# Values stage of a retrieval block: dense products for 192 of 256 tokens, gathered rows for the other 64

## The chip, the cores and the metric

The kernel runs on one core of one Trainium2 chip. The metric is the device time of one execution in microseconds (us). TensorE multiplies, ScalarE (ACT in the rows), VectorE (DVE) and GpSimd (POOL) compute and copy, and SyncE (SP) issues most transfers. In the rows PE is TensorE's matmul and PEld its weight load.

## The reference

One layer of a hybrid encoder on x of 256 tokens by 2048, all float32: token mixing (attention and retention heads), layer norm, retrieval of experts, layer norm. The change lies in the retrieval:

```
def peer_ffn(x, w_pq, sub_keys, expert_u, expert_v):
    ...
    best, pos = lax.top_k(cand, PEER_TOPK)                     # 16 experts for each of 8 heads
    expert_idx = jnp.take_along_axis(cand_idx, pos, axis=-1)   # of 16384 experts
    gate = jax.nn.softmax(best, axis=-1)
    ...
        u = jnp.take(expert_u, idx_b, axis=0)
        act = jax.nn.gelu(jnp.einsum('thkd,td->thk', u, xb), approximate=False)
        v = jnp.take(expert_v, idx_b, axis=0)
        return jnp.einsum('thk,thkd->td', g_b * act, v)
```

So each token takes 8 x 16 = 128 rows of `expert_v` (16384 rows of 2048), each with a weight gate x gelu(u . x). Then `layer_norm(ALPHA * x + ffn)`.

## The kernel before

The kernel doesn't gather. It works over all 16384 experts densely, in 128 tiles of 128 experts, for all 256 tokens. The gates are scattered into a table in DRAM that is zero elsewhere, and the weight of every expert for every token is gelu(score) x gate.

**Exact products from rounded operands.** TensorE is fed in the type fp32r. To keep float32's precision each operand is split: a high part (ScalarE's copy to fp32r) and a low part (the operand less its high part, by VectorE). A product is three matmuls, high x high, high x low and low x high, into one accumulator: the helper `three` (L443 to L445).

**Score stage** (to about 1274 us). For each tile, `expert_u` is loaded by SyncE, transposed by VectorE, split by ScalarE and VectorE, and multiplied with all tokens. ScalarE applies gelu and `wexp[:, tile, 0:256]` holds the result, experts on the partitions. Two tiles are a pair, 64 pairs in all. From pair 18 on GpSimd is free of splitting: it scatters the gates, 256 indirect transfers (`scatter`, L1818), each for 128 tokens of one block (b = 0 or 1) and one pick. Then it loads the gates of a pair (`load_gates`, L1834, two buffers) and multiplies them into `wexp` (`apply_gates`, L1842).

**Values stage** (from 1274 us). For each tile of 128 experts:
- SyncE loads the tile of `expert_v` in two halves of 1024 columns (`v_half`, L334, 512 KB each) into `raw`, four buffers. A buffer is reloaded when VectorE has split it.
- ScalarE copies the tile's weights (128 x 256) to `whalf_hi` (L1079) and each quarter (128 x 512) of the values to `split_hi` (L781), four slots. It waits until TensorE has used the slot.
- VectorE makes `whalf_lo` (L1635) and `split_lo` (L1134).
- TensorE (`value_tile`) takes each quarter for two blocks of 128 tokens, three matmuls each. Eight PSUM banks hold the sums of 2 blocks x 4 quarters over the whole stage.

Two tiles are a turn of each engine's loop. The last four tiles (`HELD`) are split into buffers of their own, so that block 0's products (`held_tile`) can all come before block 1's. **The end**: for each block VectorE adds ALPHA x residual to the sums (`summed`, L1669), takes statistics (L1672), GpSimd raises the variance to -0.5 (L1784), VectorE normalises (L1692, L1694), with some pieces by ScalarE (L1115) and GpSimd (L1776, L1777); SyncE stores eight pieces.

Each engine runs its own list in the order in which it is written, and the engines wait for each other through semaphores. An instruction that waits holds up all that stand behind it on its engine.

## Time and profile before

| | |
|---|---|
| device time, three runs | 1986.82, 1987.72, 1988.07 us, median 1987.72 |
| profiled execution | span 1986.6 us (the page states no other time of it) |
| TensorE | 99% of the span, 9838 matmuls |
| VectorE, ScalarE, GpSimd | 74%, 52%, 41% |
| DMA | 412 MB, 207 GB/s over the span |
| values, `expert_v` | 256 loads of 512 KB |
| gates | 64 loads of 256 KB |

The span runs from the first to the last instruction. The busy share of an engine is an average over stages; what bounds a stage is read from the waits in it. TensorE is the engine that waits for nobody over most of the span.

### The profile page before, as it was taken

The numbers are of one execution on the slowest core, as the hardware profiler recorded it, in microseconds if no ns is written. First come the engines' busy times: TensorE is split into PE (matmuls) and PEld (weight loads), VectorE is DVE, ScalarE is ACT, GpSimd is POOL, SyncE is SP. The second block draws the span as 40 slices with busy tenths as digits, with TensorE's granted clock in tenths as the row PEclk, the third lists the DMA queues.
The fourth block names the chain that finished last, engine by engine and source line by source line (L and its number), as shares of the span: only waits on it lengthen the run. The fifth ranks groups of instructions, "written<-read, shape, count | busy, mean of one in ns | idle before, by whom it ended". The sixth has DMA issues, their size and how long they took to land.

```text
span 1986.6 us, 37625 instructions
## 1 busy us (share of the span) xinstructions
PE 1965.2 (99%) x9838; PEld 1668.8 (84%) x9838; DVE 1478.3 (74%) x2406; ACT 1030.8 (52%) x1962; POOL 824.4 (41%) x614
## 2 busy tenths in 40 slices
PE   9999999999999999999999999999999999999996
PEld 8888888887888888888888888888888888888885
DVE  4555776766889889999999999877765555555556
ACT  4555555554655555444444444555555555555553
POOL 0000330201889998888888887456520000000001
PEclk9999999999999999999999999999999999999998
DMA  7787775676587767999999998878766555677563
GB/s 249 233 278 277 231 235 161 195 222 177 172 204 189 188 191 172 186 188 190 187 187 187 190 188 188 240 269 279 270 225 193 192 193 194 232 216 213 194 194 129
DMA packets 300843, 412.19 MB, mean 207 GB/s; under 512 B 80256, under 2 KB 211456, under 8 KB 300160
## 3 DMA queue, kind: packets, MB, share of 16 engines
q1 hardware_dynamic: 258816, 394.76, 66.4%
q0 software_dynamic: 41984, 16.93, 7.8%
q8 instruction: 18, 0.29, 0.1%
q14 instruction: 25, 0.20, 0.0%
HBM read 390.46 MB, written 21.10 MB: 207 GB/s over the span
## 4 chain that ended last, share of the span: by engine, by line
PE 96%; DVE 3%; DMA 1%; ACT 0%; POOL 0%; issue 0%; SPq 0%; DVEq 0%; ACTq 0%
PE ps L690 24%; PE ps L443 19%; PE ps L445 19%; PE ps L444 19%; PE ps L696 12%; DVE split_lo L1134 0%; PE ps L433 0%; PE ps L660 0%; DVE x_cols L1356 0%; DMA raw<-in_expert_v 0%; DVE end_lo L1662 0%; DVE act_both L1147 0%; DVE stats L1672 0%; DMA x_nat<-in_x 0%; DVE ps L1669 0%; PE ps L494 0%
## 5 line engine op out<-in xcount | busy, mean ns | idle before, releaser
L1134 DVE TENSOR_TENSOR split_lo<-raw,split_hi 128x512 fp32r<-128x512 f32 x800 | 608.3, 765 | 415.2 <-ACT split_hi L781 413.5
L781 ACT ACTIVATE split_hi<-raw 128x512 fp32r<-128x512 f32 x840 | 529.8, 632 | 545.7 <-PE ps L445 536.4
L690 PE MATMUL ps<-act_both,split_hi 128*128 128x512 f32 x2048 | 513.4, 393 | 0.0
L1818 POOL DMA_INDIRECT gate_dram<-pick_n,places x256 | 398.3, 1556 | 81.2 <-issue 81.2
L690 PEld LDWEIGHTS ps<-act_both,split_hi 128*128 128x128 f32 x2048 | 368.8, 189 | 65.4
L443 PE MATMUL ps<-split_hi,whalf_hi 128*128 128x512 f32 x992 | 386.3, 389 | 0.0
L444 PE MATMUL ps<-split_lo,whalf_hi 128*128 128x512 f32 x992 | 386.3, 389 | 0.0
L445 PE MATMUL ps<-split_hi,whalf_lo 128*128 128x512 f32 x992 | 386.3, 389 | 0.0
L992 ACT ACTIVATE split_hi<-ps 128x512 fp32r<-128x512 f32 x368 | 209.2, 595 | 260.8 <-PE ps L696 259.4
L696 PEld LDWEIGHTS ps<-act_both,split_lo 128*128 128x128 f32 x2048 | 279.5, 191 | 19.9
L696 PE MATMUL ps<-act_both,split_lo 128*128 128x256 f32 x2048 | 286.0, 283 | 0.0
L443 PE MATMUL ps<-split_hi,act_both 128*128 128x512 f32 x688 | 274.9, 400 | 1.9 <-DVE act_both L1147 1.4
L1784 POOL TENSOR_TENSOR stats<-stats 128x1 f32<-128x1 f32 (+1 forms) x6 | 9.7, 1614 | 633.2 <-DVE stats L1678 504.9
L445 PE MATMUL ps<-split_hi,act_both 128*128 128x512 f32 x688 | 268.9, 391 | 0.0
L444 PE MATMUL ps<-split_lo,act_both 128*128 128x512 f32 x688 | 268.2, 390 | 0.0
L1400 DVE TENSOR_TENSOR split_lo<-ps,split_hi 128x512 fp32r<-128x512 f32 x368 | 243.2, 680 | 16.4 <-ACT split_hi L992 11.5
L1414 DVE STREAM_TRANSPOSE ps<-raw 128x1024 f32<-128x1024 f32 x184 | 231.6, 1259 | 6.7
L444 PEld LDWEIGHTS ps<-split_lo,whalf_hi 128*128 128x128 f32 x992 | 186.2, 188 | 38.6
L445 PEld LDWEIGHTS ps<-split_hi,whalf_lo 128*128 128x128 f32 x992 | 186.2, 188 | 38.6
L443 PEld LDWEIGHTS ps<-split_hi,whalf_hi 128*128 128x128 f32 x992 | 186.2, 188 | 38.6
L1799 POOL TENSOR_TENSOR split_lo<-u_cols,split_hi 128x512 fp32r<-128x512 f32 x144 | 184.9, 1307 | 19.6 <-ACT split_hi L992 18.7
L443 PEld LDWEIGHTS ps<-split_hi,act_both 128*128 128x128 f32 x688 | 129.4, 188 | 28.0 <-DVE act_both L1147 2.1
(183 smaller groups left out, 1569.4 us busy)
## 6 DMA issues: line engine op xcount, KB each, us to landing
raw<-in_expert_u SPq DMA_DIRECT2D x1024, 128.0 KB
raw<-in_expert_v SPq DMA_DIRECT2D x256, 512.0 KB
raw<-in_w_in SPq DMA_DIRECT2D x112, 512.0 KB
gate_dram<-zeros SPq DMA_DIRECT2D x32, 512.0 KB, 5.9
raw<-in_w_out SPq DMA_DIRECT2D x32, 512.0 KB
raw<-in_w_pq SPq DMA_DIRECT2D x128, 128.0 KB
gates<-gate_dram POOLq DMA_DIRECT2D x64, 256.0 KB, 4.5
gate_dram<-pick_n,places POOLq DMA_INDIRECT x256
```

What stands on the lines that cost most here:

```text
L443: nc.tensor.matmul(acc, l_hi, r_hi, start=first, stop=False)
L444: nc.tensor.matmul(acc, l_hi, r_lo, start=False, stop=False)
L445: return nc.tensor.matmul(acc, l_lo, r_hi, start=False, stop=last)
L690: return nc.tensor.matmul(ps[:, bank, :], split_hi[:, q % SPLITS, i * P:(i + 1) * P], act_both[:, k, :, :].rearrange("p a t -> p (a t)"), ...
L696: return nc.tensor.matmul(ps[:, bank, 0:SEQ], split_lo[:, q % SPLITS, i * P:(i + 1) * P], act_hi[:, k, :], start=False, stop=False)
L781: nc.scalar.activation(split_hi[:, q % SPLITS, :], raw[:, q // 2, q % 2, :], ACT.Copy).then_inc(hi_ready, 1)
L992: nc.scalar.activation(split_hi[:, q % SPLITS, :], src, ACT.Copy).then_inc(hi_ready, 1)
L1134: vec.tensor_tensor(split_lo[:, q % SPLITS, :], raw[:, q // 2, q % 2, :], split_hi[:, q % SPLITS, :].bitcast(f32), ALU.subtract).then_inc( ...
L1400: vec.tensor_tensor(split_lo[:, q % SPLITS, :], ps[:, 4 + q % 4, :], split_hi[:, q % SPLITS, :].bitcast(f32), ALU.subtract).then_inc(lo_re ...
L1414: vec.transpose(dst.rearrange("p a (c g i) -> p g (a c) i", g=4, i=32), raw[:, k, :, :].rearrange("p a (b c q) -> p (a b) c q", b=2, c=8)) ...
L1799: eng.tensor_tensor(split_lo[:, q % SPLITS, :], u_cols[:, q // 2, q % 2, :], split_hi[:, q % SPLITS, :].bitcast(f32), ALU.subtract).then_i ...
L1818: eng.indirect_dma_start(gate_dram, bass.IndirectOffsetOnAxis(ap=places[:, b, k:k + 1], axis=0), pick_n[:, 2, b, k:k + 1], None, compute_o ...
```

## The change

The 256 tokens become a block FULL of 128 (tokens 0 to 127) and a block PART of 128, whose tokens are treated by halves.

- **Tokens 128 to 191, dense with two matmuls.** The weights of these 64 tokens stand in one operand of 128 columns, 64 low parts and 64 high parts (`wsplit`, columns LOD to LOD + 128). It is multiplied with the high and with the low values. The upper 64 rows of the bank then hold the high weights' sum, the lower 64 rows that of the low weights. (The product low x low comes with it.) At the end the lower rows are moved to the upper partitions and added.
- **Tokens 192 to 255, gathered.** Their 64 x 128 = 8192 picked rows of `expert_v` are gathered by 64 indirect transfers of 128 rows (1 MB each) into three buffers `rows`. Partitions 0 to 63 take the first 64 picks of the 64 tokens and partitions 64 to 127 the others. VectorE adds weight x row to `row_sum`, in two additions of 1024 columns for each transfer, 128 in all. The gates of these tokens aren't scattered. Their activations are stored to DRAM by SyncE during the score stage (`store_act`, four pairs behind) and picked from there by 64 small indirect transfers; GpSimd multiplies them with the gates in groups of four (`weigh`).
- Weights are applied and split for 192 columns in place of 256. ScalarE makes two copies a tile (64 and 192 columns). Gate buffers are three, and GpSimd has 16 pairs done before the first gather; from then on it weighs one pair per row.
- At the end both halves of PART are brought to their places before the sum with the residual: ScalarE copies, SyncE moves, GpSimd adds.

In the diff `store_act` is SyncE's, `add_row`, `more_rows`, the loop, `places_out` and `summed` are VectorE's, `load_row` and what follows it GpSimd's, and the last part is ScalarE's, behind its last splits.

```diff
-            def value_tile(n0, t, first, last_tile):
+            def value_product(w, q, r_hi, r_lo, b, first, last):
+                acc = ps[:, b * 4 + q, :]
+                if b == FULL:
+                    return three(acc, w[:, HI0:HI0 + P], w[:, LO0:LO0 + P], r_hi, r_lo, first, last)
+                both = w[:, LOD:LOD + P]
+                nc.tensor.matmul(acc, both, r_hi, start=first, stop=False)
+                return nc.tensor.matmul(acc, both, r_lo, start=False, stop=last)
...
+            def store_act(pair):
+                sp.wait_ge(gelu_done, pair * 2 + 2)
+                sp.dma_start(act_tiles[:, bass.ds(pair * 2, 2), :], wexp[:, bass.ds(pair * 2, 2), DENSE:SEQ]
+                             ).then_inc(act_out, 16)
...
+            def add_row(m):
+                j, cols = m // 2, slice(m % 2 * 1024, m % 2 * 1024 + 1024)
+                if m % 2 == 0:
+                    dve.wait_ge(row_in[j % ROW_SLOTS], 16 * (j // ROW_SLOTS + 1))
+                    dve.wait_ge(weight_ready, j // W_GROUP + 1)
...
+                vec.scalar_tensor_tensor(out=row_sum[:, cols], in0=rows[j % ROW_SLOTS][:, cols], scalar=picked_w[:, j:j + 1],
+                                         in1=row_sum[:, cols], op0=ALU.mult, op1=ALU.add).then_inc(row_used, 1)
+            def more_rows(i, at):
+                turn = i - FIRST_STEP
+                due = turn >= 0 and (at < 2 or turn % 5 == 4)
+                if due and done < 2 * STEPS:
+                    add_row(done)
+                    done += 1
...
+            for i in range(loops):
                 split_w(i * 8, 1)
                 for q in range(4, 8):
                     split(i * 8 + Q_V, q)
+                    if q == 5:
+                        more_rows(i, 0)
+                more_rows(i, 2)
                 split_w(i * 8, 2)
                 for q in range(4):
                     split(i * 8 + (Q_V + 8), q)
+                    if q == 1:
+                        more_rows(i, 1)
...
             def places_out():
+                chain.step(vec.scalar_tensor_tensor(out=places_f[HB:P, 0, :], in0=pick_n[HB:P, 0, PART, :], scalar=float(P),
+                                                    in1=pick_n[HB:P, 1, PART, :], op0=ALU.mult, op1=ALU.add))
...
+                vec.tensor_copy(places_u[HB:P, :, :], places_f[HB:P, :, :]).then_inc(places_ready, 1)
...
             dve.wait_ge(x1_out, 16)
+            dve.wait_ge(picked_in, 64)
...
+                    def load_row(j):
+                        if j >= ROW_SLOTS:
+                            pool.wait_ge(row_used, 2 * (j - ROW_SLOTS) + 2)
+                        eng.indirect_dma_start(rows[j % ROW_SLOTS][:, :], None, v_rows,
+                                               bass.IndirectOffsetOnAxis(ap=picked[:, 0, j:j + 1], axis=0)
+                                               ).then_inc(row_in[j % ROW_SLOTS], 16)
...
+                    for pair in range(APPLIED_AHEAD):
+                        apply_gates(pair)
+                    pool.wait_ge(split_free, Q_V + SPLITS)
+                    for j in range(ROW_SLOTS):
+                        load_row(j)
+                    eng.memset(row_sum[HB:P, :], 0.0).then_inc(own_ready, 1)
...
+                    eng.tensor_scalar(row_sum[0:HB, :], row_sum[0:HB, :], ALPHA, None, ALU.mult).then_inc(own_ready, 1)
+                    pool.wait_ge(act_out, 16 * PAIRS)
+                    load_acts(0)
+                    weigh(0)
+                    load_acts(1)
+                    pair = APPLIED_AHEAD
+                    for k in range(W_GROUPS):
+                        for j in range(k * W_GROUP + ROW_SLOTS, min((k + 1) * W_GROUP + ROW_SLOTS, STEPS)):
+                            load_row(j)
+                            if pair < PAIRS:
+                                apply_gates(pair)
+                                pair += 1
+                        if k + 1 < W_GROUPS:
+                            weigh(k + 1)
+                        if k + 2 < W_GROUPS:
+                            load_acts(k + 2)
...
             def summed(b, q):
-                dve.wait_ge(values_ready, 4 * b + q + 1)
+                if b == PART:
+                    dve.wait_ge(own_rows, q + 1)
+                    dve.wait_ge(low_added, q + 1)
...
+            act.wait_ge(row_used, 2 * STEPS)
+            for q in range(2):
+                low_to_sbuf(q)
+            act.wait_ge(own_summed, 1)
+            for q in range(2):
+                own_to_psum(q)
+            for q in range(2, 4):
+                low_to_sbuf(q)
+            for q in range(2, 4):
+                own_to_psum(q)
```

Other places in words. In the last four tiles the weights are in `wend`, and PART's products come before FULL's. SyncE loads the residual of tokens 192 to 255 into `row_sum` at the start of the values stage, moves `row_sum`'s upper half down (`half_moved`) after the last value load, and moves the four pieces of low sums. `DENSE` is 192, `HB` 64, `STEPS` 64, `ROW_SLOTS` 3, `W_GROUP` 4, `FIRST_STEP` 2. VectorE's and GpSimd's loops of the values stage are written out.

TensorE in the values loop, the matmuls of one quarter. Before, `whalf_hi` and `whalf_lo` are the weights:

```order
L443 MATMUL ps<-split_hi,whalf_hi 128x512
L444 MATMUL ps<-split_lo,whalf_hi 128x512
L445 MATMUL ps<-split_hi,whalf_lo 128x512
L443 MATMUL ps<-split_hi,whalf_hi 128x512
L444 MATMUL ps<-split_lo,whalf_hi 128x512
L445 MATMUL ps<-split_hi,whalf_lo 128x512
```

After, L507 to L509 are `three` and L794, L795 the two with the mixed operand. One matmul of six is gone:

```order
L507 MATMUL ps<-split_hi,wsplit 128x512
L508 MATMUL ps<-split_lo,wsplit 128x512
L509 MATMUL ps<-split_hi,wsplit 128x512
L794 MATMUL ps<-split_hi,wsplit 128x512
L795 MATMUL ps<-split_lo,wsplit 128x512
```

VectorE in the values loop, one tile and the start of the next, before:

```order
L1635 TENSOR_TENSOR whalf_lo<-wexp,whalf_hi 128x256
L1133 REGISTER_ALU
L1134 TENSOR_TENSOR split_lo<-raw,split_hi 128x512
L1133 REGISTER_ALU
L1134 TENSOR_TENSOR split_lo<-raw,split_hi 128x512
L1133 REGISTER_ALU
L1134 TENSOR_TENSOR split_lo<-raw,split_hi 128x512
```

After, a turn with a third addition (L1751 is the addition, L1227 the split of the values, L1738 that of the weights; the number behind `rows` names the buffer):

```order
L1738 TENSOR_TENSOR wsplit<-wexp,wsplit 128x192
L1227 TENSOR_TENSOR split_lo<-raw,split_hi 128x512 x2
L1751 SCALAR_TENSOR_TENSOR row_sum<-rows_108,picked_w,row_sum 128x1024
L1227 TENSOR_TENSOR split_lo<-raw,split_hi 128x512 x2
L1751 SCALAR_TENSOR_TENSOR row_sum<-rows_108,picked_w,row_sum 128x1024
L1738 TENSOR_TENSOR wsplit<-wexp,wsplit 128x192
L1227 TENSOR_TENSOR split_lo<-raw,split_hi 128x512 x2
L1751 SCALAR_TENSOR_TENSOR row_sum<-rows_109,picked_w,row_sum 128x1024
```

An addition of 1024 columns now stands in the middle of each tile's four splits, and every fifth turn has one between the tiles.

GpSimd in the values stage, before:

```order
L1842 TENSOR_TENSOR wexp<-wexp,gates_59 128x512
L1843 REGISTER_ALU
L1834 ISA
L1834 DMA gates_59<-gate_dram 128x512
L1840 ISA
L1842 ISA
L1842 TENSOR_TENSOR wexp<-wexp,gates_60 128x512
L1834 ISA
L1834 DMA gates_60<-gate_dram 128x512
```

After, the border between two groups of four rows (L1999 gathers a row for each partition, L1990 and L1982 weigh a pair and load the gates of a later one, L2014 makes four weights of the next group, L2006 picks activations):

```order
L1999 DMA rows_107<-in_expert_v,picked 128x2048
L1990 TENSOR_TENSOR wexp<-wexp,gates_60 128x2x192
L1982 DMA gates_60<-gate_dram 128x2x192
L2014 TENSOR_TENSOR picked_w<-picked_act,picked_gate 128x4
L2006 DMA picked_act<-act_dram,picked 128x1 x4
L1999 DMA rows_108<-in_expert_v,picked 128x2048
```

The weights of a group now stand behind a gather and a gate multiply, and that gather waits until VectorE has used the row three before.

## Rows read from the trace of the kernel before

**Rows 1.** The page: span, TensorE's busy time, and the chain's shares by engine

```profile
span 1986.6 us, 37625 instructions
PE 1965.2 (99%) x9838; PEld 1668.8 (84%) x9838; DVE 1478.3 (74%) x2406; ACT 1030.8 (52%) x1962; POOL 824.4 (41%) x614
PE 96%; DVE 3%; DMA 1%; ACT 0%; POOL 0%; issue 0%; SPq 0%; DVEq 0%; ACTq 0%
```

**Rows 2.** Timeline, TensorE, first matmuls of the values stage and of its last tiles

```profile
1274.24 0.40 PE L443 MATMUL ps<-split_hi,whalf_hi 128*128 128x512 f32 x1
...
1948.82 0.40 PE L443 MATMUL ps<-end_hi,wend_hi 128*128 128x512 f32 x1
```

**Rows 3.** Busy time by stretch: score stage, values stage thrice; last PEclk, DMA share, GB/s

```profile
840.00:1240.00 400.00, 400.00 (x2294) 352.26 (x2293) 382.83 (x503) 196.39 (x428) 329.61 (x212) 1.00 0.93 188
1310.00:1400.00 90.00, 90.00 (x399) 74.53 (x398) 67.61 (x82) 47.35 (x83) 52.64 (x55) 1.00 0.82 274
1500.00:1600.00 100.00, 100.00 (x443) 82.81 (x442) 56.87 (x92) 52.64 (x92) 0.00 (x0) 1.00 0.59 193
1824.00:1828.00 4.00, 4.00 (x19) 3.31 (x18) 1.64 (x4) 2.01 (x5) 0.00 (x0) 1.00 0.95 357
```

**Rows 4.** Waits 1274 to 1948 us: who for whom, us in total, times, longest

```profile
ACT split_hi L781 <- PE ps L445: 313.4, 487, 0.8
DVE split_lo L1134 <- ACT split_hi L781: 252.3, 440, 1.8
```

**Rows 5.** Groups by line, VectorE's splits, 1274 to 1461 and 1461 to 1600 us

```profile
L1134 DVE TENSOR_TENSOR split_lo<-raw,split_hi 128x512 fp32r<-128x512 f32 x139 | 128.6, 934 | 47.0 <-ACT split_hi L781 46.4
...
L1134 DVE TENSOR_TENSOR split_lo<-raw,split_hi 128x512 fp32r<-128x512 f32 x103 | 72.0, 700 | 58.4 <-ACT split_hi L781 58.3
```

**Rows 6.** VectorE back to back (timeline), and L1346 by its line (ns min/median/max)

```profile
1944.85 1.43 DVE L1656 TENSOR_TENSOR wend_lo<-wexp,wend_hi 128x256 fp32r<-128x256 f32 x4
1946.19 4.90 DVE L1662 TENSOR_TENSOR end_lo<-raw,end_hi 128x512 fp32r<-128x512 f32 x8
...
L1346 DVE SCALAR_TENSOR_TENSOR x_nat<-x_nat,stats,ln_w x5: 744/1274/1282, 445.8 to 462.9; 128x1024 f32<-128x1024 f32 x3, 128x512 f32<-128x512 f32 x2
```

**Rows 7.** Timeline, GpSimd: the last of 256 indirect issues

```profile
1235.65 1.55 POOL L1818 DMA_INDIRECT gate_dram<-pick_n,places  x1 [0.30 <-issue]
```

**Rows 8.** Timeline of the same time: VectorE, then GpSimd

```profile
1339.05 2.17 DVE L1134 TENSOR_TENSOR split_lo<-raw,split_hi 128x512 fp32r<-128x512 f32 x2 [0.67 <-ACT split_hi L781]
...
1344.49 0.69 DVE L1134 TENSOR_TENSOR split_lo<-raw,split_hi 128x512 fp32r<-128x512 f32 x1 [0.33 <-ACT split_hi L781]
...
1338.78 1.28 POOL L1842 TENSOR_TENSOR wexp<-wexp,gates 128x512 f32 x1 [0.41 <-DMA gates<-gate_dram]
...
1344.28 0.55 POOL L1834 DMA_DIRECT2D gates<-gate_dram  x1 [0.67 <-DMA gates<-gate_dram]
```

**Rows 9.** DMA: GB/s in 1-us slices of 1790:1830; q0 in 840:1240; issues to landing

```profile
GB/s 115 225 258 94 238 228 203 76 54 202 221 246 373 385 360 283 221 127 303 123 209 246 111 250 188 98 279 227 156 61 58 190 165 176 336 393 397 303 295 90
...
q0 software_dynamic: 30768, 0.12, 20.7%
...
x_back<-x_dram SPq DMA_DIRECT2D x16, 128.0 KB, 4.2
...
ln2b<-in_ln_b SPq DMA_DIRECT2D x1, 1024.0 KB, 8.7
```

**Rows 10.** The tail: timeline of ScalarE and VectorE; GpSimd's groups by line

```profile
1956.95 2.42 ACT L1111 ACTIVATE end_hi<-raw 128x512 fp32r<-128x512 f32 x4 [2.49 <-DMA raw<-in_expert_v]
...
1960.09 0.69 DVE L1669 SCALAR_TENSOR_TENSOR ps<-x_back,ps 128x512 f32<-128x512 f32 x1
...
1965.54 0.26 DVE L1677 BATCH_NORM_AGGREGATE stats<-stats 128x2 f32<-128x24 f32 x1
...
L1776 POOL TENSOR_TENSOR y_out<-y_out,ln2w 128x512 f32<-128x512 f32 x3 | 3.8, 1281 | 2.7 <-ACT y_out L1115 2.7
...
L1784 POOL TENSOR_TENSOR stats<-stats 128x1 f32<-128x1 f32 x2 | 1.1, 558 | 504.9 <-DVE stats L1678 504.9
```

257 lines of the change are left out of this document (181 added, 76 removed).

## The prediction

> **What bounds the kernel now.** I read the head of the page first, then the chain that ended last, then the engines by stretch, then the waits. [rows 1]: TensorE is busy 99% of the span and is 96% of the chain, so in every long stage it sets the time. [rows 2]: the values stage begins at 1274.24 and its last tiles at 1948.82 us. In between stand 62 turns of two tiles, 48 matmuls each, 2976 in all, so one costs 674.58 / 2976 = 0.2267 us and a turn 10.88 us. [rows 3]: no stretch of it leaves TensorE idle and the granted clock is 1.00, the 2.4 GHz level, so nothing is to be had from the clock. VectorE is at 57% when GpSimd rests and 75% when GpSimd weighs gates; DMA is at 0.59 and 0.82 of its time. [rows 4]: the waits are the feeders' own: ScalarE waits 313.4 us for TensorE to free a slot, VectorE 252.3 us for ScalarE. TensorE waits for nobody. Fewer matmuls therefore mean a shorter stage, until one of the feeders is full.
>
> **What is removed.** Five matmuls per quarter in place of six: three for the 128 tokens, two for the 64. In the turns that is 62 x 8 = 496 fewer: 496 x 0.2267 = **-112.4 us**, a turn then takes 9.07 us. I assume that a matmul with the mixed weights costs what the others do, since its shape is the same. The last four tiles also lose 16 matmuls (3.6 us), but the first block's products there wait for the last operands: the last of VectorE's splits ends at 1960.1 [rows 10] and the second block's 48 products come after it either way. I count 0 and keep -3.6 as a bound.
>
> **What VectorE gets.** Work in a turn of 9.07 us: eight splits of 128x512. Back to back they take 4.90 / 8 = 0.61 us, alone 0.69 [rows 6, 5]. Two weight splits, 192 columns now; four of 256 take 1.43 us, 0.36 each, and by the columns 0.29. And 2.2 additions of 128x1024. The nearest row is the same operation and shape with its operands in SBUF, 1274 ns median [rows 6]; back to back less the same 0.08, so 1.20. Sum 8 x 0.61 + 2 x 0.29 + 2.2 x 1.20 = **8.1 us**; with every duration taken alone 8 x 0.69 + 2 x 0.35 + 2.2 x 1.27 = 9.0.
>
> On top comes GpSimd. [rows 5]: the same split takes 934 ns while gates are weighed and 700 after. [rows 8] show why: two splits that overlap a GpSimd multiply take 2.17 us, one that overlaps GpSimd's issue of a transfer takes 0.69, as always. So the multiply costs a busy VectorE some 0.7 us, the issue nothing. The multiply shrinks from 512 to 384 columns, 0.5 us of delay, 1.1 of them a turn: +0.55 us, in the 44 turns in which the 48 remaining pairs are weighed.
>
> A wait is added too. The weights of a group of four rows are multiplied by GpSimd only after it has waited for the last row of the group before to be used. Behind that stand a gather (1.55 + 0.30 us, the pace of indirect issues in [rows 7]), a gate multiply (1.28 for 512 columns [rows 8], about 1.0 for 384), the wait and the issue of a gate load (0.67 + 0.55 [rows 8]) and the weights' own multiply (0.56, a tiny one on GpSimd [rows 10]): 4.6 us. The next addition is due about 4.5 - 1.2 = 3.3 us after the last ended. VectorE, with the splits queued behind the addition, waits 1.3 us every 3.6 turns: +0.4 a turn. Together 8.1 + 0.55 + 0.4 = 9.07 us, all of the turn. VectorE is full, just.
>
> The Trainium skill has a rule against this edit: the page Vector Engine (DVE) Microarchitecture Reference, "Points that are easy to get wrong", says that this operation with two sources in SBUF that aren't bf16 runs at half throughput. By it an addition would cost 1.07 us more. The row of this kernel with two such sources disagrees: 1274 ns for 1024 columns is one column per 1.04 ns plus a start.
>
> **What the queues get.** A turn loads four blocks of 512 KB, 1.1 gathers of 1 MB and 1.1 gate loads of 192 KB: 2.10 + 1.15 + 0.22 = 3.47 MB, 382 GB/s at 9.07 us. Before, 274 GB/s is the most that any long stretch moves, at a share of 0.82; 357 GB/s stand in one of 4 us at 0.95 [rows 3]; slices of 1 us reach 385 and 397 [rows 9]. So DMA is nearly full too. At 375 GB/s, between the last two, a turn is 9.25 us. By the long stretch alone, 274 / 0.82 = 334 GB/s, it is 10.4; at 397 it costs nothing.
>
> Three resources at 97 to 100% don't mesh without loss, since a slot of four gives a split less than 2 us of slack (4 x 1.13, less 1.13 and the 1.4 of both splits). I take 9.4 us for the 44 turns with gates and 9.07 for the rest: 44 x 0.33 = **+14 us** (0 to +38 here; more is a rival).
>
> **Start of the additions: +3 us (0 to 7).** GpSimd issues its last scatter at 1235.65 [rows 7] and, two landings of some 4 us [rows 9] later, weighs 16 pairs at 2.2 us or more (1.0 + 0.67 + 0.55). It then issues three gathers, clears and scales the sum (2048 columns; at most 5.1 us for the scaling by the 1.28 of 512), issues four small gathers and waits for them: about 1304. VectorE comes to the first addition about 1295, with up to 2 us of slack. The scatters of the second block have half the rows; if that makes them shorter, the stall is gone.
>
> **Score stage: +1.5 us (0 to 6).** Three more small VectorE instructions and a wait for four copies. The stores of 64 tokens' activations (64 x 256 short packets) come into a stretch where DMA is at 0.93 and TensorE still has no gap [rows 3]; the scatters there, 20.7% of the 16 engines' time [rows 9], shrink by a quarter and make room.
>
> **Tail: +5 us (2 to 9).** Today VectorE begins the end of the first block at 1960.1 and is through at 1965.5 [rows 10]; from there it works without a gap. Now ScalarE copies the low half out, but only after its last splits (1956.95 + 2.42 [rows 10]), a transfer moves it across partitions (4.2 us, like the residual's [rows 9]), GpSimd adds it (1.3 a piece [rows 10]), four times. First sum about 1965, last 1970.7: 5 us late, and the second block stands behind it on VectorE.
>
> **Sum.** On the profiled span: 1986.6 - 112.4 + 14 + 3 + 1.5 + 5 = 1897.7; the median shown is 1.1 above that span, so **1899 us**.
>
> **Rivals.**
> - *TensorE stays the bound, the feeders keep up.* For it: with VectorE at 96% of the stretch 840 to 1240, TensorE has no gap there [rows 3]. 1987.7 - 112.4 + 5 = 1880, 1877 with the saving in the last tiles.
> - *The queues are the bound.* At 357 GB/s a turn is 9.72: 58 turns x 0.65 = 38 us in place of 14, 1923; at 334 GB/s 58 x 1.33 = 77, 1962. For it: no stretch longer than 4 us has shown more. Against: share and rate don't rise together, 1 us slices reach 397. The skill's HBM Reference ("Specifications (TRN2)") gives a core 358 GB/s as its share and about 425 when it streams alone. The one would be this rival at 1923, the other would leave DMA out of the matter; only one core runs here, and the 397 is above the share.
> - *Slower: the gathers' issue holds VectorE up.* No row shows VectorE reading two SBUF tensors beside an indirect issue of 1.55 us; the direct issue of 0.55 beside it costs nothing [rows 8]. There are 2.2 indirect issues a turn (a gather and an activation's per row). If each blocked VectorE in full, a turn were 9.07 + 3.4 = 12.5: 58 x 3.4 = 200 us, 2085 and slower. It turns into a loss from about 10.9 us a turn, 0.8 us per issue.
> - *The rows come too late.* Three slots of 8 KB give a gather two rows' time, 16.5 us; a load of 1 MB landed in 8.7 [rows 9]. Beyond some 18 us VectorE waits at each row; beyond 23 the gain is gone.
> - *The addition at half rate,* as the page has it: 128 x 1.07 = 137 us more on a full VectorE, 2035.
>
> **How the numbers follow.** Forecast 52%, TensorE bound 15%, queues 18%, issue 10%, late rows 4%, half rate 1%. The range is 1877 to 1962 us: both bounds of the DMA rate and the free case; it leaves the last three out. 0.2% (4 us) is about what a measurement can tell from no change. Faster 0.87, same 0.02, slower 0.11.
>
> **What would show it.** Matmuls of the stage still 0.227 us apart where they run, with 5 per quarter. TensorE with idle time released by VectorE's split, some 15 us in all, nearly all of it while gates are weighed. VectorE above 95% until then; its addition at 1.27 us. DMA share above 0.9. If ScalarE waits for the values' load instead, it is the queues; if splits take over 1 us after the last gate, it is the issue; if the addition waits for the row, the gather is late. A tail that is not longer, or a stall of tens of us at the first addition, would make terms wrong, not the sign.

## The result, and the profile after

The changed kernel takes 1973.0 us in the median of 4 runs (1968.5 to 1977.5), the kernel before 1987.9 (1986.8 to 1989.8). The ratio is 0.9926, 95% interval 0.9914 to 0.9937. So it is 15 us faster, where 89 were forecast, and outside the range of 1877 to 1962. The profiled execution is the slowest of the four, 1977.5 us with a span of 1975.7. I compare it with the span of 1986.6 before, so the rows account for 11 us of the 15 and show some 4 us more loss than the median has.

The head of the page and the chain's shares, which answer [rows 1]:

```profile
span 1975.7 us, 36205 instructions
PE 1887.2 (96%) x9326; PEld 1574.4 (80%) x9326; DVE 1600.8 (81%) x2538; ACT 1031.9 (52%) x2098; POOL 1002.3 (51%) x770
PE 66%; issue 12%; POOL 11%; DMA 4%; DVE 4%; SPq 2%; ACT 1%; POOLq 0%; ACTq 0%; DVEq 0%
```

TensorE has 512 matmuls less (9838 to 9326), 496 of them in the turns, as counted. But it is 66% of the chain and no longer 96%. The busy time by stretch, which answers [rows 3] (busy us and count of PE, PEld, DVE, ACT, POOL; then granted clock, DMA share, GB/s):

```profile
840.00:1240.00 400.00, 400.00 (x2295) 352.25 (x2294) 382.93 (x502) 196.83 (x429) 325.63 (x226) 1.00 0.92 195
1274.00:1300.00 26.00, 13.51 (x51) 10.65 (x50) 8.73 (x15) 7.71 (x19) 13.26 (x8) 0.74 0.82 263
1300.00:1740.00 440.00, 408.88 (x1717) 317.49 (x1716) 386.04 (x519) 243.31 (x516) 221.76 (x198) 1.00 0.93 333
1740.00:1860.00 120.00, 102.39 (x403) 80.02 (x402) 86.65 (x124) 56.70 (x121) 33.71 (x30) 0.91 0.90 292
1860.00:1930.00 70.00, 69.16 (x304) 56.56 (x303) 59.97 (x93) 43.64 (x97) 8.57 (x7) 1.00 0.86 308
```

The score stage is as it was. In the values stage TensorE is starved in three places: at the start (half idle, and the granted clock falls to 0.74), all through 1300 to 1740, and from 1740 to 1860, where the clock falls too. Only from 1860 on does it run nearly without a gap. The waits from 1310 to 1740 (who for whom: us in total, times, longest), which answer [rows 4]:

```profile
POOL rows L1999 <- DVE row_sum L1751: 181.5, 37, 9.6
ACT split_hi L851 <- PE ps L795: 98.3, 152, 5.3
ACT split_hi L851 <- DMA raw<-in_expert_v: 92.4, 54, 4.0
PEld ps L507 <- DVE split_lo L1227: 58.7, 74, 3.9
DVE split_lo L1227 <- ACT split_hi L851: 42.6, 45, 2.7
DVE row_sum L1751 <- issue: 7.6, 5, 3.5
```

ScalarE waits 92 us for the values' loads, and TensorE for VectorE. So no single engine is the bound. GpSimd and "issue" (time for which the profile names no releaser) together are 23% of the chain, but GpSimd isn't full either: of the 430 us it waits 181.5 for VectorE to use a row. A count makes the loss plain. VectorE splits every value once, 496 splits in the loop, eight to a turn, and at TensorE's pace of 9.07 us a turn a split stands for 1.134 us. The groups by line, 1310 to 1740 us and 1740 to 1860 us, which answer [rows 5]:

```profile
L1227 DVE TENSOR_TENSOR split_lo<-raw,split_hi 128x512 fp32r<-128x512 f32 x334 | 242.5, 762 | 42.8 <-ACT split_hi L851 42.6
L1751 DVE SCALAR_TENSOR_TENSOR row_sum<-rows,picked_w,row_sum 128x1024 f32<-128x1024 f32 x92 | 120.2, 1307 | 8.0 <-issue 7.6
...
L1227 DVE TENSOR_TENSOR split_lo<-raw,split_hi 128x512 fp32r<-128x512 f32 x82 | 56.3, 719 | 33.3 <-ACT split_hi L851 33.2
```

334 splits in 430 us are a turn of 10.30 us, and 430 - 334 x 1.134 = 51 us are lost. 82 splits in 120 us lose 27. From 1270 to 1310 there are 22 in 40 us, 15 lost, and some 3 are left for the time after 1860 and the borders between the stretches. With 5 us in the tail: 1986.6 - 112.4 + 15 + 51 + 27 + 3 + 5 = 1975. The forecast had +14 for meshing, +3, +1.5 and +5 in their place.

**The start.** SyncE's queue and, last, VectorE's first split after the gap:

```profile
1263.56 2.86 SPq L366 DMA_DIRECT2D raw<-in_expert_v  x2
1266.47 9.21 SPq L421 DMA_DIRECT2D act_dram<-wexp  x4
1275.78 13.26 SPq L441 DMA_DIRECT2D row_sum<-x_dram  x8
1289.41 2.17 SPq L366 DMA_DIRECT2D raw<-in_expert_v  x4
...
1294.05 3.02 DVE L1227 TENSOR_TENSOR split_lo<-raw,split_hi 128x512 fp32r<-128x512 f32 x4 [14.09 <-ACT split_hi L851]
```

The last four stores of activations and the eight loads of the residual are new on SyncE and stand ahead of the values' next loads. Together they hold its queue for 22.5 us, and VectorE idles for 14.1. Not all of it is issue: for 7.5 of the 9.2 us of the stores SyncE waits until ScalarE has made the last activations. VectorE has split the first slot's values at 1273, so what holds back its reload until 1289.4 is above all the residual's eight loads, 13.3 us; one of them alone takes 6.05.

**A group's weights.** VectorE, then GpSimd at the same time:

```profile
1458.50 1.32 DVE L1751 SCALAR_TENSOR_TENSOR row_sum<-rows,picked_w,row_sum 128x1024 f32<-128x1024 f32 x1 [3.55 <-issue]
...
1453.75 2.07 POOL L1999 DMA_INDIRECT rows<-in_expert_v,picked  x1 [3.94 <-DVE row_sum L1751]
...
1458.19 0.21 POOL L2014 TENSOR_TENSOR picked_w<-picked_act,picked_gate 128x4 f32<-128x4 f32 x1
```

The gather, the gate's multiply and the gate's load stand before the weights' multiply, 4.4 us, and the addition starts 0.1 us after it. This is the wait that the forecast took from the order of the code.

**The residual for the end.** The chain from 1737.5 us (start, us, what):

```profile
1737.52 0.38 SPq L463
...
1737.95 2.44 SPq L463
...
1740.43 3.67 SPq L463
...
1744.14 0.58 SPq L463
...
1745.08 3.21 SPq L366
...
1748.54 7.32 DMA raw<-in_expert_v
...
1755.96 0.64 ACT split_hi L851
```

Four loads of 128 KB, in pieces of 128 bytes, hold SyncE's queue for 7.2 us. The issue of the values' load behind them, 0.33 us otherwise, takes 3.21, and the transfer 7.32. ScalarE had waited for it.

**The tail.** SyncE, GpSimd, and VectorE's first sum, which answer [rows 10]:

```profile
1929.23 6.79 SPq L366 DMA_DIRECT2D raw<-in_expert_v  x5
1936.07 0.52 SPq L470 DMA_DIRECT2D row_half<-row_sum  x1
...
1945.91 4.58 POOL L2047 TENSOR_TENSOR row_sum<-row_sum,row_half 64x2048 f32<-64x2048 f32 x1 [49.60 <-DMA row_half<-row_sum]
...
1952.00 0.69 DVE L1807 SCALAR_TENSOR_TENSOR ps<-x_back,ps 128x512 f32<-128x512 f32 x1 [5.94 <-POOL x_back L2052]
```

From the end of the loop's splits (1929.2) to the end of the span are 46.5 us, before 41.7 (1944.9 to 1986.6): 4.8 more. VectorE idles 5.9 us before the first sum. GpSimd is late because the transfer of the sum's upper half was issued behind five of the values' loads and took 9.8 us.

### The profile page after: what moved, and what is told of

It is laid out like the page before. It is cut to its first block, busy times and chain, and to the rows that moved or that the text cites. A ratio compares the mean times of both kernels' runs of the same rounds, so it can differ in the third digit from the quotient of the medians.

```text
span 1975.7 us, 36205 instructions
## 1 busy us (share of the span) xinstructions
PE 1887.2 (96%) x9326; PEld 1574.4 (80%) x9326; DVE 1600.8 (81%) x2538; ACT 1031.9 (52%) x2098; POOL 1002.3 (51%) x770
## 4 chain that ended last, share of the span: by engine, by line
PE 66%; issue 12%; POOL 11%; DMA 4%; DVE 4%; SPq 2%; ACT 1%; POOLq 0%; ACTq 0%; DVEq 0%
PE ps L754 24%; PE ps L760 12%; PE ps L507 9%; PE ps L509 9%; PE ps L508 9%; POOL rows L1999 3%; DMA raw<-in_expert_v 3%; POOL wexp L1990 3%; POOL picked_act L2006 3%; POOL gates L1982 2%; DVE split_lo L1227 1%; SPq L463 1%; PE ps L795 1%; PE ps L794 1%; SPq L441 1%
## 5 line engine op out<-in xcount | busy, mean ns | idle before, releaser
L1227 DVE TENSOR_TENSOR split_lo<-raw,split_hi 128x512 fp32r<-128x512 f32 x800 | 585.0, 755 | 269.0 <-ACT split_hi L851 267.3
L851 ACT ACTIVATE split_hi<-raw 128x512 fp32r<-128x512 f32 x840 | 518.3, 629 | 533.7 <-PE ps L509 218.9
L1958 POOL DMA_INDIRECT gate_dram<-pick_n,places x256 | 380.4, 1486 | 78.1 <-issue 77.8
L760 PEld LDWEIGHTS ps<-act_both,split_lo 128*128 128x128 f32 x2048 | 279.5, 190 | 19.9
L507 PE MATMUL ps<-split_hi,act_both 128*128 128x512 f32 x688 | 274.7, 399 | 2.0 <-DVE act_both L1240 1.5
L509 PE MATMUL ps<-split_hi,act_both 128*128 128x512 f32 x688 | 268.7, 391 | 0.0
L507 PE MATMUL ps<-split_hi,wsplit 128*128 128x512 f32 x496 | 206.2, 416 | 62.1 <-DVE split_lo L1227 60.4
L1999 POOL DMA_INDIRECT rows<-in_expert_v,picked x64 | 92.2, 1441 | 296.7 <-DVE row_sum L1751 291.5
L508 PE MATMUL ps<-split_lo,wsplit 128*128 128x512 f32 x496 | 196.8, 397 | 0.0
L509 PE MATMUL ps<-split_hi,wsplit 128*128 128x512 f32 x496 | 196.4, 396 | 0.0
L794 PE MATMUL ps<-split_hi,wsplit 128*128 128x512 f32 x496 | 196.0, 395 | 0.0
L795 PE MATMUL ps<-split_lo,wsplit 128*128 128x512 f32 x496 | 195.5, 394 | 0.0
L1938 POOL TENSOR_TENSOR split_lo<-u_cols,split_hi 128x512 fp32r<-128x512 f32 x144 | 184.8, 1310 | 19.6 <-ACT split_hi L1062 18.9
L507 PEld LDWEIGHTS ps<-split_hi,wsplit 128*128 128x128 f32 x496 | 94.6, 191 | 113.0 <-DVE split_lo L1227 95.9
L1751 DVE SCALAR_TENSOR_TENSOR row_sum<-rows,picked_w,row_sum 128x1024 f32<-128x1024 f32 x128 | 166.2, 1298 | 9.2 <-issue 8.7
```

Source lines behind the costliest of these rows:

```text
L507: nc.tensor.matmul(acc, l_hi, r_hi, start=first, stop=False)
L508: nc.tensor.matmul(acc, l_hi, r_lo, start=False, stop=False)
L509: return nc.tensor.matmul(acc, l_lo, r_hi, start=False, stop=last)
L760: return nc.tensor.matmul(ps[:, bank, 0:SEQ], split_lo[:, q % SPLITS, i * P:(i + 1) * P], act_hi[:, k, :], start=False, stop=False)
L794: nc.tensor.matmul(acc, both, r_hi, start=first, stop=False)
L795: return nc.tensor.matmul(acc, both, r_lo, start=False, stop=last)
```

## The experiments

In the table are the splits of VectorE in three stretches of each profile, read like the rows above. In brackets stands what the stretch lost against 1.134 us a split. In e4, e9, e10 and e13 TensorE has less to do, so a loss there can be below 0. Those four, e1 and e2 ran once, e5, e6 and e7 twice, the others four times. The four runs of a kernel lie 4 to 12 us apart, and each kernel has one profile: the changed kernel, e5, e6 and e7 of their slowest run, e8 of its fastest. A difference of a few us, or of 3 or 4 splits, therefore proves nothing by itself.

| kernel | time, us | 1270 to 1310 | 1310 to 1740 | 1740 to 1860 |
|---|---|---|---|---|
| after | 1973.0 | 22 (15) | 334 (51) | 82 (27) |
| e1 thin additions | 1937.6 | 22 (15) | 355 (27) | 94 (13) |
| e2 quarter rows | 1935.9 | 20 (17) | 352 (31) | 102 (4) |
| e5 both | 1912.6 | 21 (16) | 366 (15) | 106 (0) |
| e4 two products of five out | 1962.4 | 25 (12) | 331 (55) | 93 (15) |
| e9 e1 and e4 | 1934.0 | 24 (13) | 352 (31) | 92 (16) |
| e10 e2 and e4 | 1927.7 | 23 (14) | 349 (34) | 106 (0) |
| e13 e10, quarter loads | 1911.7 | 25 (12) | 358 (24) | 113 (-8) |
| e6 whole pieces | 1964.8 | 21 (16) | 334 (51) | 90 (18) |
| e7 no gates' multiply | 1965.0 | 19 (18) | 341 (43) | 84 (25) |
| e3 start order | 1968.6 | 26 (11) | 332 (54) | 92 (16) |
| e8 merged | 1954.4 | 29 (7) | 336 (49) | 96 (11) |
| e11 merged, quarter loads | 1936.4 | 27 (9) | 341 (43) | 102 (4) |
| e12 quarter loads alone | 1964.5 | 21 (16) | 340 (44) | 85 (24) |

### e1 and e2: VectorE or the queues

e1, the additions over 8 columns:

```
-                j, cols = m // 2, slice(m % 2 * 1024, m % 2 * 1024 + 1024)
+                j, cols = m // 2, slice(m % 2 * 1024, m % 2 * 1024 + 8)
```

> The changed kernel, with each of VectorE's 128 additions over 8 columns in place of 1024 (so the sum of the gathered rows is left out for the other columns); all gathers and waits as they are. It takes some 150 us of work off VectorE and no byte off DMA. Theory A (the queues bound the stage, at about 340 GB/s): no more than 15 us faster than the changed kernel's 1973 us, ScalarE still waits over 120 us for the values' load. Theory B (VectorE is full): 1890 to 1910 us, and the waits for the load go to nearly nothing.

e2, only every fourth row gathered:

```
+                        if j >= ROW_SLOTS and j % 4:
+                            eng.dma_start(rows[j % ROW_SLOTS][:, 0:8], v_rows[0:P, 0:8]).then_inc(row_in[j % ROW_SLOTS], 16)
+                            return
                         eng.indirect_dma_start(rows[j % ROW_SLOTS][:, :], None, v_rows,
```

> The changed kernel, with only every fourth gather carried out; in place of the others GpSimd issues a load of 32 bytes per partition into the same buffer, so those rows' sums are left out. VectorE's additions keep their full size. It takes some 46 of 67 MB off DMA. Theory A (queues): 1905 to 1925 us, that is, all but the stall at the start of the stage and the tail comes back, and ScalarE waits less than 40 us for the values' load. Theory B (VectorE is full): within 15 us of 1973.

Measured: 1937.6 and 1935.9 us, 35 and 37 less than 1973. Both expectations of both runs missed. Neither VectorE nor the queues is the bound alone. The two profiles in the stretch 1300 to 1740, e1 then e2:

```profile
1300.00:1740.00 440.00, 425.82 (x1818) 340.48 (x1818) 312.81 (x552) 255.72 (x545) 194.72 (x207) 0.99 0.96 354
```

```profile
1300.00:1740.00 440.00, 422.20 (x1803) 333.70 (x1802) 410.03 (x545) 262.28 (x541) 211.60 (x203) 1.00 0.80 269
```

With thin additions the queues go to a share of 0.96. With fewer rows VectorE goes to 410 of 440 us. Each takes up what the other gave.

### e5: both reliefs

Both edits together.

> Both reliefs at once: the additions cover 8 columns in place of 1024, and after the first three only every fourth row is gathered (the rest are 32-byte loads), so the result lacks most of the picked rows' sum. Each alone gave about 36 us (1937.6 and 1935.9). Theory: VectorE and the DMA queues are both near full and each keeps the other from making good a delay, so together they give back nearly all of what the forecast missed: a turn of 9.1 to 9.3 us, TensorE bound, 1893 to 1908 us with the late start and the slow stretch from 1740 to 1860 left in. Rival: something that neither relieves (GpSimd's multiply on the gates, the order on SyncE, the 128-byte pieces) holds the turn at 9.4 to 9.7 us: 1920 to 1935.

Measured: 1912.6 us (1910.8 and 1914.5), between the two ranges, nearer to the theory's. The stretches 1300 to 1740 and 1740 to 1860:

```profile
1300.00:1740.00 440.00, 431.16 (x1868) 351.26 (x1868) 320.32 (x567) 270.28 (x559) 181.98 (x211) 0.99 0.83 278
1740.00:1860.00 120.00, 119.64 (x528) 98.68 (x528) 83.00 (x160) 76.63 (x158) 18.15 (x23) 1.00 0.79 262
```

From 1740 on there are 106 splits in 120 us, a turn of 9.06 us: TensorE's own pace, as the forecast had it. So the saving of 112.4 us is real. SyncE's short pieces are still there, and cost nothing when VectorE and the queues have room. The table says which of the two matters more here: with fewer rows alone (e2) the stretch loses 4 us, with thin additions alone (e1) 13. What is left is the start (16 us), 15 us from 1310 to 1740, and the tail.

### e4: TensorE relieved

```
-                    for b in range(TB):
+                    for b in ([FULL, PART] if first else [FULL]):
```

> The changed kernel without the two matmuls for the 64 mixed tokens in the loop after its first tile, so their sums are left out: three matmuls per quarter, 24 x 0.227 = 5.4 us a turn in place of 9.07. All loads, splits and additions stay. Theory A (queues at 340 GB/s, 3.47 MB a turn): a turn can't get below some 9.7 to 10 us, the time stays within 30 us of 1973. Theory B (VectorE, 8.1 us of work a turn and more with GpSimd beside it): 40 to 90 us faster. If the queues lose only by their meshing with TensorE's pace, also faster, with a rate of over 370 GB/s over the stage.

Measured: 1962.4 us, 11 less, in one run. From 1310 to 1740 there are 331 splits, no more than in the changed kernel (334). The 11 us lie within the 30 that the theory of the queues allowed, and outside the 40 to 90 of the other. TensorE's 9.07 us don't hold that stretch at all.

### e9 and e10: each of the two by itself

e9 is e1 and e4 together: only the queues are left near a limit. e10 is e2 and e4 together: only VectorE.

> The queues measured by themselves: additions over 8 columns, and the two products of the low and high weights left out in the loop, so that VectorE has some 6.5 us and TensorE 5.4 us of work in a turn while all loads and gathers stay (the result lacks both parts). Theory (the queues carry 355 to 365 GB/s at most when both kinds of load are always waiting): 3.47 MB take 9.5 to 9.8 us, 350 to 362 splits from 1310 to 1740 us, as with thin additions alone (355), 1925 to 1938 us. Rival (the forecast's 375 GB/s or more was there and the other engines kept the queues from it): 372 splits or more, below 1915.

> VectorE measured by itself: every fourth row gathered after the first three (other rows: 32-byte loads), and the two products of the low and high weights left out in the loop; the additions are whole (the result lacks both parts). DMA has 2.6 MB a turn and TensorE 5.4 us of work. Theory (the forecast's sum for VectorE, 9.07 us a turn with GpSimd's multiply and the wait for a group's weights, is about right, and quarter rows alone were slower because three engines near their limits disturb one another): 362 to 379 splits from 1310 to 1740 us, 1900 to 1920 us. Rival (VectorE's own work is longer than summed, 9.7 us a turn): 350 to 356 splits, as with quarter rows alone (352), 1928 to 1938.

Measured: 1934.0 and 1927.7 us. e9, the DMA view from 1310 to 1740, and from the waits of the same stretch ScalarE's for loads:

```profile
DMA packets 45196, 154.00 MB, mean 358 GB/s; under 512 B 14272, under 2 KB 14272, under 8 KB 38790
```

```profile
ACT split_hi L851 <- DMA raw<-in_expert_v: 142.1, 77, 5.8
```

e9's theory held. With nothing else to wait for, the queues carry 358 GB/s, 352 splits, a turn of 9.77 us. e1 has 355 splits, so thin additions alone had already brought the kernel to the queues' limit. In e10 neither held, but the rival missed by very little (349 splits against 350 to 356, 1927.7 us against 1928 to 1938, a turn of 9.86 us). But its rows don't say that VectorE's work is that long (stretch, then wait):

```profile
1300.00:1740.00 440.00, 315.31 (x1079) 210.28 (x1078) 399.52 (x544) 247.76 (x540) 238.13 (x202) 0.92 0.79 268
```

```profile
ACT split_hi L851 <- DMA raw<-in_expert_v: 108.8, 69, 5.9
```

VectorE is busy 399.5 of 440 us, and ScalarE waits 109 us for loads although the queues are at 0.79. That left open what holds a turn when both have room.

### e11, e12, e13: when a load is released

A values' load of 512 KB fills one of four slots, and is issued when both splits of the slot's last content are done. The edit loads quarters of 256 KB, each as soon as its own split is done, with a second set of semaphores for the odd quarters:

```
-                sp.dma_start(raw[:, slot, :, :].rearrange("p a b -> p (a b)"),
-                             v_v[bass.ds(j * P, P), hf * 1024:hf * 1024 + 1024]).then_inc(raw_ready[slot], 16)
+                for a in range(2):
+                    if free is not None:
+                        sp.wait_ge(lo_ready, free + a)
+                    sp.dma_start(raw[:, slot, a, :], v_v[bass.ds(j * P, P), hf * 1024 + a * COLS:hf * 1024 + a * COLS + COLS]
+                                 ).then_inc((raw_ready, raw_odd)[a][slot], 16)
```

e11 has it on the merged kernel (e8, below), e12 on the changed kernel, e13 on e10.

> Complete kernel, on top of the merged one (1954.4 median): the values' loads come as 256 KB (512 columns, 2 KB pieces) in place of 512 KB, each issued as soon as its own quarter is split instead of when both are. Theory (the loss from 1310 to 1740 is a lack of slack: a load has 6 us between its slot's release and its use, and lands in 5 to 6 us while a gather runs): a load gets a split's time more, 1.1 us, 345 to 355 splits there in place of 336, 1937 to 1948 us. Rival (queues near their ceiling and shorter pieces cost them more than slack gives): at most 338 splits, 1953 us or more.

> Complete kernel: the changed kernel with the values' loads in quarters of 256 KB (2 KB pieces) as its only edit. On the merged kernel the same edit took 18 us (1954.4 to 1936.4). Theory (a good part of what the change fails to bring is lost because a values' load is released too late, in every stretch of the stage): 12 to 22 us less than 1973, 1951 to 1961. Rival (in the merged kernel the quarters helped because the start, the residual's loads and the weights were already out of the way): 1966 or more.

> VectorE alone, as in the tenth run (a quarter of the rows gathered, two products of five left out, whole additions: 349 splits from 1310 to 1740 us, 1927.7 us), with the values' loads in quarters of 256 KB. There VectorE was busy 399.5 of 440 us although the queues were at 0.79 and TensorE had little to do. Theory (VectorE's own work fits in 9.1 to 9.3 us a turn, the rest of the 9.86 is loads released late): 365 splits or more, VectorE busy over 415 of 440 us, 1900 to 1912 us. Rival (VectorE's instructions and waits themselves take the 9.86 us): at most 355 splits, 1920 us or more.

Measured: e11 1936.4 us (1936.1 to 1946.9), 18 less than e8, better than its theory's range in time and short of it in splits (341). e12 1964.5 (1962.5 to 1966.1), 8.5 less than the changed kernel: a clear gain, since its slowest run is faster than the changed kernel's fastest, but between the theory's 12 to 22 and the rival's bound of 7. e13 1911.7, 16 less than e10, in one run, in the theory's range (1900 to 1912) by a hair; its 358 splits lie between the two, and VectorE's 413.9 us just under the 415. e13, the stretch and the waits:

```profile
1300.00:1740.00 440.00, 318.71 (x1107) 208.87 (x1105) 413.91 (x561) 260.63 (x553) 248.72 (x209) 0.94 0.86 275
```

```profile
ACT split_hi L855 <- DMA raw<-in_expert_v: 66.1, 49, 5.5
DVE row_sum L1757 <- issue: 14.4, 8, 2.3
```

The same work takes 9.61 us a turn in place of 9.86, and ScalarE's wait falls from 109 to 66 us. Why it matters is seen best in the chain of the merged kernel from 1740 us:

```profile
1740.17 8.19 DMA raw<-in_expert_v
...
1748.47 0.64 ACT split_hi L864
...
1749.13 1.31 DVE split_lo L1240 x2
...
1750.45 9.16 DMA raw<-in_expert_v
```

VectorE's splits release a slot, the load takes 8.19 us to land, two splits follow, and the slot is released again, 10.28 us after the first time. No engine works without a break in that loop. The four slots are used once a turn, so a turn can't be shorter than one slot's round. At 9.07 us the round leaves 7.1 us for issue and landing. The loads in the chain take 7.3 to 9.4 us in the changed kernel (six of them from 1748 to 1868 us), 6.1 to 13.0 in the merged one (from 1328 us on). From 1300 to 1740 us the merged kernel's chain is 31% such loads and 23% splits. The chain picks out the slow loads, and the profile gives no landing time for all of the 512 KB loads, so what share of the rounds is too long stays open. The quarters of e11 land in 6.4 us (median of all) and start a split earlier. The edit changes two things at once, the time of the release and the size of a load, and no run has one without the other; nor did any run have a fifth slot.

### e3, e8: a mended start, and the merged kernel

e3 puts the values' loads ahead of the stores and the residual's pieces on SyncE, one of each in turn, weights the first group before the sum is scaled, and lets the additions begin in turn 4:

```
-            for pair in range(PAIRS - STORE_LAG, PAIRS):
-                store_act(pair)
...
+                v_half(i * 2 + n // 2, n % 2, n)
+                if i == 1:
+                    store_act(PAIRS - STORE_LAG + n)
...
+                own_piece(RAWS * (i - 1) + n)
```

> The changed kernel with another order at the start of the values stage: SyncE issues each load of values of the first two turns ahead of one of the last activation stores and one piece of the residual, GpSimd picks and multiplies the first weights before it scales the sum, and the additions start two turns later (a third one in every fourth turn). Theory: the 14 us in which ScalarE waits for the first reload of the values after 1280 us, behind 13 us of residual pieces on SyncE, go; 1957 to 1963 us if nothing takes its place. Rival (the stage is bound by DMA bytes alone, so the loads only come later): 1968 to 1978, no change.

Measured: 1968.6 us in the median, but 1962.7 to 1974.9, so 4.4 less than the changed kernel, which the spread of both doesn't tell from nothing; two runs of four came near the expected 1957 to 1963, two did not. In its profile the start loses 11 us in place of 15: the loads are ahead now, but each residual piece still holds SyncE between two of them.

e8 adds three things: the weights one row into the group before, the residual's 16 loads one by one between the values' loads, and the sum's upper half ahead of the last four loads:

```
-                        if k + 1 < W_GROUPS:
-                            weigh(k + 1)
+                            if j == k * W_GROUP + ROW_SLOTS and k + 1 < W_GROUPS:
+                                weigh(k + 1)
...
+                v_half(i * 2 + k // 2, k % 2, k)
+                if n % 2:
+                    back_piece(n // 2)
...
+                if n == 4:
+                    sp.wait_ge(row_used, 2 * STEPS)
+                    sp.dma_start(row_half[0:HB, :], row_sum[HB:P, :]).then_inc(half_moved, 16)
```

> Complete kernel. On top of the start order of the third experiment (1968.6 median, 1961.9 span of the profile): a group's weights are multiplied one row into the group before instead of at its end; the residual's 16 loads are issued one by one between the values' loads instead of four in a row; the row that carries the upper half of the sum is issued before the last four values' loads. Theory: the wait for a group's weights goes (about 9 us of VectorE's idle time, half of which shows), the stretch 1740 to 1860 gains 5 to 8 us, the tail 3 to 5: 1950 to 1957. Rival: queues and VectorE stay full, only the tail gains: 1962 to 1967.

Measured: 1954.4 us (1949.0 to 1960.4), ratio to the kernel before 0.9837 (0.9810 to 0.9865). The time is in the theory's range, but not all of its parts came. The tail gained 0.5 us and not 3 to 5: from the end of the loop's splits to the end of the span are 45.9 us (1901.3 to 1947.2), against 46.4 in e3. The sum's upper half comes sooner, but it is put ahead of the last four values' loads, and VectorE's last split ends 19.9 us after the loop's, 3 us later than in e3. From 1310 to 1740 us VectorE has no wait for a group's weights left. Yet the stretch has 336 splits, hardly more than 334. The wait had been 7.6 us, but the loads are as late as before (ScalarE waits 86.0 us for them, against 92.4), and 6.0 us of idle time before splits, for which the profile names no releaser, are new. The start loses 7 us and the stretch from 1740 on 11.

e11, on top of it, has the ratio 0.9758 (0.9729 to 0.9786): 51 us faster than the kernel before and 37 faster than the changed one. Its stretches:

```profile
1300.00:1740.00 440.00, 417.76 (x1754) 323.63 (x1752) 407.95 (x530) 253.78 (x526) 232.95 (x201) 1.00 0.97 342
1740.00:1860.00 120.00, 117.30 (x505) 93.58 (x505) 106.27 (x156) 73.72 (x152) 35.92 (x31) 1.00 1.02 357
```

### e6 and e7: two smaller causes

e6, the residual's loads in long pieces:

```
-                        sp.dma_start(natural[:, r, :, :], strided(x1_dram[of_rows, b, cols])[:, r, :, :]
+                        sp.dma_start(x1_back[to_rows.start + r * n:to_rows.start + r * n + n, b, cols], v_v[r * n:r * n + n, cols]
```

> The residual's 16 loads for the end, which come in pieces of 128 bytes, are replaced by 16 loads of the same size in pieces of 4 KB from the values' first rows (wrong content, same bytes). In the changed kernel the stretch 1740 to 1860 us has 82 splits of VectorE, against 93 at the pace of the stretch before it. Theory (the short pieces occupy the queues, and SyncE's 1.3 to 1.8 us an issue hold back the values' loads behind them): 91 to 95 splits there and 10 to 15 us less, 1958 to 1963. Rival (it is their bytes, or the two tables of 1 MB before them): at most 85 splits there and within 4 us of 1973.

e7, the gates' multiply in 4 columns:

```
-                        part = wexp[:, 2 * pair:2 * pair + 2, 0:DENSE]
+                        part = wexp[:, 2 * pair:2 * pair + 2, 0:DENSE if pair < APPLIED_AHEAD else 4]
...
```

> GpSimd's multiply on the gates covers 4 of 192 columns in the 48 pairs of the values stage; the gates' loads stay, the result lacks those gates. With the multiply VectorE's splits take 762 ns on average from 1310 to 1740, without it about 690. Theory (the multiply's hold on VectorE is a part of the loss): 334 x 0.07 = 23 us less work for VectorE and, since the queues hold the other part, 8 to 20 us faster: 1953 to 1965. Rival (the queues set the pace there): within 5 us of 1973.

Measured: e6 1964.8 us (1959.9 and 1969.7), 90 splits from 1740 to 1860. That is inconclusive: e3 and e4, with their short pieces in place, have 92 and 93 there, and e7 and e12 84 and 85. So kernels whose edits lie elsewhere differ here by 10 splits, 11 us. That may be scatter from run to run and most of the spread between a kernel's runs; no kernel was profiled twice, so it isn't shown. What e6 does show is the issue. SyncE's instruction in the changed kernel and in e6 (ns min/median/max):

```profile
L463 SPq DMA_DIRECT2D x_back<-x_dram x16: 382/754/3666, 1737.5 to 1816.4; - x16
```

```profile
L463 SPq DMA_DIRECT2D x_back<-in_expert_v x16: 337/431/1530, 1739.5 to 1809.7; - x16
```

e7 gave 1965.0 us (1960.6 and 1969.4), 8 less, at the edge of the theory's range; its slower run lies among the changed kernel's. The splits take 686 ns in place of 762 from 1310 to 1740, 341 of them. GpSimd's multiply does slow VectorE, but is at most a small part of the loss. The splits and the stretch:

```profile
L1227 DVE TENSOR_TENSOR split_lo<-raw,split_hi 128x512 fp32r<-128x512 f32 x341 | 222.3, 686 | 74.3 <-ACT split_hi L851 64.9 <-issue 8.5
```

```profile
1310.00:1740.00 430.00, 404.70 (x1718) 320.41 (x1717) 348.97 (x520) 239.28 (x513) 179.03 (x195) 0.99 0.95 345
```

## Why the prediction was wrong, point by point

- **TensorE's saving, -112.4 us: right.** 496 matmuls fewer, and e5 has the turn of 9.06 us in its last stretch. TensorE is simply no longer what sets the pace.
- **VectorE's work in a turn: 3% short.** Forecast 8.65 us busy and 0.4 of waiting for weights, 9.05 (the forecast writes 9.07). In the changed kernel it is 386.0 / 440 x 10.30 = 9.04 busy and 7.6 us / 41.75 turns = 0.18 waiting, and with the most room (e13) 9.04 and 0.32. So a turn takes up to 9.36 us for VectorE, not 9.07. That is 13 us over 44 turns. The term that was too small is GpSimd's multiply. In e7, nearly without it, VectorE is busy 349.0 of 430 us, 8.19 us a turn of 10.09: the 8.1 for its own work held, and the multiply costs some 0.9 us where 0.55 was put.
- **The addition at half rate: didn't happen.** The 92 additions from 1310 to 1740 us take 1307 ns on average. By the rule of the Trainium skill it would have been 1.07 us more (Vector Engine (DVE) Microarchitecture Reference, "Points that are easy to get wrong"); these rows don't bear it out.
- **The issue of gathers holding up VectorE, and rows too late: didn't happen.** In e7, nearly without the multiply, the splits are at 686 ns beside all those issues, and in the changed kernel they are at 687 from 1770 on, after the last gate's multiply. All six waits before an addition end 0.1 us after the weights' multiply, and no row shows an addition waiting for its row.
- **The queues' rate: the step that failed by its number.** "At 375 GB/s, between the last two" took the rate from slices of 1 us. Held for 430 us with both kinds of load always waiting, it was 358 (e9), a turn of 9.77 us in place of 9.25. The bytes were right: 144.8 MB in 41.75 turns are 3.47 MB each. Over the 44 turns that load gates the half microsecond is 23 us. The rival at 357 GB/s, 1923 us with a chance of 18%, had the rate right. Its 38 us counted gate loads in all 58 turns; without them a turn has 3.25 MB, 9.1 us at that rate, so the rate alone costs 44 x 0.70 = 31 us, the loss that e9 shows. The Trainium skill's HBM Reference ("Specifications (TRN2)"), which gives a core a share of 358 GB/s, has the same figure; I had set it against a slice of 397. That section of the Trainium skill also gives about 425 for a core that streams alone; here it wasn't reached, though the queues' share in e9 was 0.97. That one core alone stops there for that reason isn't shown by any run.
- **The +14 us for the turns with gates (0 to 38): the term that failed most, by the rate and by meshing.** From 1310 to 1740 the loss is 51 us. The 14 were 44 x 0.33, of which 0.18 a turn, 8 us, stood for the queues' rate and 6 for meshing. If the queues' 31 are taken off the 51, some 20 are left for meshing: so 23 of the 37 us of error are the rate's and 14 meshing's. That division is an estimate. With TensorE relieved, the queues alone lose 31 there (e9), VectorE alone 34 (e10), and the two together 55 (e4). I read it so: a delay by one isn't made good while the other is near its limit. The forecast had seen that "a slot of four gives a split less than 2 us of slack" and priced it as small. It had not written down the round of a slot: release, issue, landing, two splits. It knew no landing time of a values' load, and took none. e11, e12 and e13 show that smaller loads, released earlier, gain 18, 8.5 and 16 us with the same work, and that even so 24 to 44 of the us up to 1740 stay lost.
- **The start, +3 us: wrong by 12, and the step missing.** I followed GpSimd's queue and not SyncE's. The diff puts 12 transfers ahead of the values' loads there. They hold its queue for 22.5 us, 13.3 of them with the residual's pieces. The +3 had been for the first addition, before which VectorE shows no idle time.
- **The stretch from 1740, not costed: 27 us.** The forecast took 9.07 us a turn here, without loss. The residual's loads were there before, under TensorE's cover. With that cover gone, 7.2 us of SyncE and the late load behind them come through. How much of the 27 is due to the pieces stays open: 0 to 4 wherever fewer rows are gathered (e5, e10, e2), 11 with the loads spread (e8), 18 with long pieces (e6), where the kernels with this code and all gathers and additions lie between 15 and 27. In the slower ones the clock falls as well (0.91 in the changed kernel), and I can't separate its price.
- **Score stage, +1.5 us: nothing.** TensorE has no gap from 840 to 1240 us, and its DMA share is 0.92.
- **The tail, +5 us: 4.8, by luck, for another reason.** Not ScalarE's copies and the four moved quarters alone, but first the transfer of the sum's upper half, issued too late on SyncE.

The sign was right. The error on the span is 78 us (1975.7 against 1897.7): 37 from 1310 to 1740, 27 from 1740 on, 12 at the start, the rest small. The size failed on a transfer rate taken from slices of 1 us, and on two shared things that the sum treated one by one: the slots' round, through which VectorE and the queues delay each other, and SyncE's queue.

## What to carry to other kernels

When a change fills three resources to 97% or more, write down the round of the buffer that joins them: release, issue, landing under load, use. If that round is longer than the new pace, it is the bound, whatever the busy shares say. Take a transfer rate from a stretch as long as the one that is forecast, at a share near 1, never from the best microsecond. And for each transfer that a diff adds, read what stands behind it on the same issuing queue. Transfers that are harmless under a bound elsewhere can come to the surface when that bound is lifted.

## What the runs showed of the hardware

- Loads in 4 KB pieces and gathered 8 KB rows, with the gates' loads beside them, together moved 358 GB/s over 430 us on one core (e1 and e9 alike, at a share of 0.97).
- An issue on SyncE isn't of fixed length. The values' load takes 0.33 us (all 166 from 1310 to 1740), but 3.21 behind four loads of 128-byte pieces; those take 0.38 to 3.67 us each, against 0.34 to 1.53 with 4 KB pieces.
- Quarter loads in 2 KB pieces moved 342 GB/s at a share of 0.97, where 4 KB pieces reached 354 at 0.96 (e11, e1). The shorter pieces cost a little rate; the time gained all the same.
- Indirect issues on GpSimd, a gather of a row and four small ones per group beside them, didn't slow VectorE's splits: they take 686 ns in e7, beside 46 gathers and 47 small ones. GpSimd's multiply of 128x384 did, to 762 ns on average (after).
